# One engine makes both parts of the filler weights, eight chunks ahead, in a one-core two-layer kernel

## The reference

```python
h = rms_norm(x, w)
swa_q, swa_k, swa_v, swa_gate, mla_q, c_kv, k_rope, mla_gate, mem_q, mem_gate = split(h @ w_in)
out_swa = attention(norm(swa_q), norm(swa_k), swa_v, bias, window) * silu(swa_gate)
kv      = rms_norm(c_kv, kv_norm) @ w_kv_up
out_mla = attention(rope(norm(mla_q)), rope(norm([kv, k_rope])), kv) * silu(mla_gate)
out_mem = attention(norm(mem_q), norm(mem @ w_k), mem @ w_v) * silu(mem_gate)
x = x + concat(out_swa, out_mla, out_mem) @ w_out
```

## Time and profile before

| | us |
|---|---|
| median of 3 runs | 2868.59 (2864.26 to 2870.82) |
| profiled execution, whole time | 2862.06 |
| its span | 2860.3 |
| PE busy | 2573.9 |
| DVE busy | 1334.4 |
| ACT busy | 1087.0 |
| POOL busy | 511.7 |

### The profile page before, as it was taken

How to read it: one execution, slowest core, us unless ns; L and a number is a source line. 1 busy time by engine, 2 the same in 40 slices (tenths; PEclk the granted TensorE clock), 3 DMA queues, 4 the chain that set the end, 5 groups by cost and what they waited for, 6 DMA issues and landing times. The chain is left out here.

```text
span 2860.3 us, 39591 instructions
## 1 busy us (share of the span) xinstructions
PE 2573.9 (90%) x14740; PEld 1873.2 (65%) x14740; DVE 1334.4 (47%) x2501; ACT 1087.0 (38%) x1922; POOL 511.7 (18%) x411
## 2 busy tenths in 40 slices
PE   8999999998888889999989999677889988978888
PEld 7984556886544444459957768565678767756667
DVE  5654784664211112347745545533435433474443
ACT  5553122443222122235434224344445344434444
POOL 0000110020011100010000000555530065064332
PEclk9999999999999999999999999898899989999999
DMA  7754344553599999945420135322244533432332
GB/s 300 220 205 152 134 145 144 184 199 123 239 422 422 422 421 422 380 187 179 172 81 32 46 126 197 119 103 103 103 148 150 177 114 115 147 118 104 130 116 107
DMA packets 80320, 529.77 MB, mean 185 GB/s; under 512 B 9088, under 2 KB 13568, under 8 KB 18848
## 3 DMA queue, kind: packets, MB, share of 16 engines
q1 hardware_dynamic: 76128, 514.50, 47.5%
q0 software_dynamic: 3456, 11.02, 1.5%
q10 hardware_dynamic: 576, 2.10, 0.2%
HBM read 520.24 MB, written 7.34 MB: 184 GB/s over the span
## 5 line engine op out<-in xcount | busy, mean ns | idle before, releaser
L798 POOL TENSOR_TENSOR parts_wl<-ring,parts_wh 128x512 fp32r<-128x512 f32 x288 | 396.3, 1395 | 1160.8 <-ACT parts_wh L783 1156.0
L759 PE MATMUL ps<-parts_wh,layer_xh 128*128 128x512 f32 x576 | 251.6, 437 | 107.8 <-POOL parts_wl L798 45.1
L2302 PE MATMUL ps<-ring,yT 128*64 128x256 f32 x2048 | 247.7, 386 | 52.6 <-DMA ring<-in_weights 48.5
L783 ACT ACTIVATE parts_wh<-ring 128x512 fp32r<-128x512 f32 x288 | 175.9, 629 | 276.9 <-PE ps L761 260.5
L760 PE MATMUL ps<-parts_wl,layer_xh 128*128 128x512 f32 x576 | 240.1, 417 | 0.0
L761 PE MATMUL ps<-parts_wh,layer_xl 128*128 128x512 f32 x576 | 239.6, 416 | 0.0
L2302 PEld LDWEIGHTS ps<-ring,yT 128*64 128x64 f32 x2048 | 137.7, 137 | 155.6 <-DMA ring<-in_weights 91.2
L1169 PE MATMUL ps<-ring,xT 128*128 128x512 f32 x512 | 222.0, 592 | 2.8 <-PEq L488 1.7
L759 PEld LDWEIGHTS ps<-parts_wh,layer_xh 128*128 128x128 f32 x576 | 117.3, 204 | 149.4 <-issue 58.6
L413 DVE TENSOR_TENSOR split_wl<-ring,split_wh 128x512 fp32r<-128x512 f32 x208 | 145.3, 709 | 96.5 <-ACT split_wh L387 95.4
L456 ACT ACTIVATE features_wh<-ring 128x512 fp32r<-128x512 f32 x208 | 130.3, 631 | 133.3 <-PE ps L473 133.3
(11 more groups left out here) (671 smaller groups left out, 5328.9 us busy)
## 6 DMA issues: line engine op xcount, KB each, us to landing
ring<-in_weights SPq DMA_DIRECT2D x468, 1024.0 KB, 5.0
x_res<-in_x SPq DMA_DIRECT2D x1, 2048.0 KB, 7.6
yT<-in_mem SPq DMA_DIRECT2D x1, 2048.0 KB, 15.7
rel_skew<-lru_feat POOLq DMA_DIRECT2D x1, 2048.0 KB, 49.8
mem_features<-yT ACTq DMA_DIRECT2D x4, 512.0 KB, 6.9
s_wb<-in_s_bc POOLq DMA_DIRECT2D x4, 512.0 KB, 3.9
s_wc<-in_s_bc POOLq DMA_DIRECT2D x4, 512.0 KB, 3.9
gate_bias<-in_gate_bias POOLq DMA_DIRECT2D x8, 256.0 KB, 3.9
```

Source lines behind the costliest of these rows:

```text
L759: mm(out, xh[:, kc, at], wh[:, c, :], start=kc == 0, stop=False)
L783: k.nc.scalar.activation(k.parts[0][:, c, :], k.ring[:, slot, c * BLK:(c + 1) * BLK], ACT.Copy).then_inc(w_high.sem, 1)
L798: k.nc.gpsimd.tensor_tensor(k.parts[1][:, c, :], k.ring[:, slot, c * BLK:(c + 1) * BLK], k.parts[0][:, c, :], ALU.subtract)\
L2302: last = nc.tensor.matmul(k.ps[s * WIN:(s + 1) * WIN, p, 0:FF], window[:, p, kc, :], k.ring[:, slot, at:at + FF], start=kc == 0, stop=kc = ...
```

## The change

- `LEAD` and the depth of the high parts go from 4 to 8 chunks (`LATE_DEEP`), in the late `gemm_tokens` stages too. The low part is written over the raw chunk in the ring (`k.w_low` lies where the ring's four slots lie), so in those stages the slot is given back by PE's last use and no longer by DVE's.
- In `SplitFill`, ACT makes no high parts: GpSimd makes the high part, waits for it, and makes the low part. `highs` is empty.
- `SmallProduct` gives way to `KeyProduct`: 96 fp32r matmuls of 64 columns, run on PE inside `rms_scale`; GpSimd splits its weights beside the `gemm_tokens` stage.
- The `gemm_tokens` of 2 column blocks in `mla_branch` is gone. Its 32 steps go into the fills: the sliding-window fill has 80 steps (latent inputs 64, half of the gate 16), the latent fill 80 (16 of the gate, 64 as before).
- Steps by block: even layer 24, turns of 16, 16, 16 and 8, then 16, memory 8, turns of 8, 8. Sliding window 16, 8, turns of 12, 8. Latent 16, 16, turns of 8, 16. Odd memory 8, turns of 8, 8.
- In `attention`, DVE evicts a filler block of slot 1 after the mixing and no longer ahead of it; `head_norm` can evict one early.

```diff
-        wh, wl = (k.sb(scope, f"split_w{n}", [P, deep, BLK], F32R) for n in "hl") if parts is None else parts
+        deep = LATE_DEEP if late else SPLIT_DEEP
+        if not late:
+            wh, wl = (k.sb(scope, f"split_w{n}", [P, deep, BLK], F32R) for n in "hl")
 
         def raw(unit, turn, c):
             return k.ring[:, slot_of(unit, turn, 2 * upb), c * BLK:(c + 1) * BLK]
+
+        def high(j, kc):
+            return k.w_high[:, (j * chunks + kc) % deep, :] if late else wh[:, kc % deep, :]
+
+        def low(unit, turn, j, kc):
+            c = kc % UNIT_KC
+            return k.w_low[:, slot_of(unit, turn, 2 * upb), c * BLK:(c + 1) * BLK] if late else wl[:, kc % deep, :]
...
+                            if late and c == UNIT_KC - 1:
+                                mid.then_inc(k.unit_used, 1)
...
-                        dve.drain().then_inc(k.unit_used, 1)
+                            nc.vector.tensor_tensor(low(unit, turn, j, kc), raw(unit, turn, c), high(j, kc), ALU.subtract).then_inc(w_low.sem, 1)
+                        if not late:
+                            dve.drain().then_inc(k.unit_used, 1)
...
-    LEAD = SPLIT_DEEP
+    LEAD = LATE_DEEP
...
     def highs(self, act, steps):
-
-        if self.act_done < len(self.blocks):
-            self.make_highs(act, min(self.act_at + steps, self.first[self.act_done + 1] + self.LEAD))
-
-    def make_highs(self, act, upto):
-        k, x_high, w_high, w_used = self.k, self.k.ev("x_high"), self.k.ev("w_high"), self.k.ev("w_used")
-        for step in range(self.high_at, min(upto, self.total)):
-            while self.act_done < len(self.blocks) and self.first[self.act_done + 1] <= step - self.LEAD:
-                self.take_act(act)
-            act.wait_ge(w_used.sem, w_used.at(step - SPLIT_DEEP))
-            coming = self.raw_piece(step)
-            if coming is not None:
-                n, _, piece = coming
-                k.nc.scalar.activation(self.blocks[n][0][0][:, piece, :], self.blocks[n][4][:, piece, :], ACT.Copy).then_inc(x_high.sem, 1)
-            slot, c = unit_wait(k, act, self.base + step // UNIT_KC, 0, 0), step % UNIT_KC
-            k.nc.scalar.activation(k.parts[0][:, c, :], k.ring[:, slot, c * BLK:(c + 1) * BLK], ACT.Copy).then_inc(w_high.sem, 1)
-            self.high_at = step + 1
+        pass
 
     def lows(self, pool, steps):
-        k, x_high, x_low, w_high, w_low = (self.k, *(self.k.ev(n) for n in ("x_high", "x_low", "w_high", "w_low")))
+        k, copy, minus = self.k, self.k.nc.gpsimd.tensor_copy, self.k.nc.gpsimd.tensor_tensor
+        x_high, x_low, w_high, w_low, w_used = (k.ev(n) for n in ("x_high", "x_low", "w_high", "w_low", "w_used"))
         self.pool_at += steps
         for step in range(self.low_at, min(self.pool_at + self.LEAD, self.total)):
+            pool.wait_ge(w_used.sem, w_used.at(step - self.LEAD))
             coming = self.raw_piece(step)
             if coming is not None:
                 n, m, piece = coming
                 (xh, xl), raw = self.blocks[n][0], self.blocks[n][4]
+                copy(xh[:, piece, :], raw[:, piece, :]).then_inc(x_high.sem, 1)
                 pool.wait_ge(x_high.sem, x_high.at(m))
-                k.nc.gpsimd.tensor_tensor(xl[:, piece, :], raw[:, piece, :], xh[:, piece, :], ALU.subtract).then_inc(x_low.sem, 1)
-            slot, c = slot_of(self.base + step // UNIT_KC, 0, 0), step % UNIT_KC
+                minus(xl[:, piece, :], raw[:, piece, :], xh[:, piece, :], ALU.subtract).then_inc(x_low.sem, 1)
+            slot, c = unit_wait(k, pool, self.base + step // UNIT_KC, 0, 0), step % UNIT_KC
+            high, raw_w, at = k.w_high[:, step % self.LEAD, :], k.ring[:, slot, c * BLK:(c + 1) * BLK], slice(c * BLK, (c + 1) * BLK)
+            copy(high, raw_w).then_inc(w_high.sem, 1)
             pool.wait_ge(w_high.sem, w_high.at(step))
-            k.nc.gpsimd.tensor_tensor(k.parts[1][:, c, :], k.ring[:, slot, c * BLK:(c + 1) * BLK], k.parts[0][:, c, :], ALU.subtract)\
-                .then_inc(w_low.sem, 1)
+            minus(k.w_low[:, slot, at], raw_w, high, ALU.subtract).then_inc(w_low.sem, 1)
             self.low_at = step + 1
...
+    def split(self, pool):
+        k, high = self.k, self.k.ev("small_high")
+        pool.wait_ge(k.loaded, k.loads)
+        k.nc.gpsimd.tensor_copy(self.high[:, :, :], self.raw).then_inc(high.sem, 1)
+        pool.wait_ge(high.sem, high.at(0))
+        k.nc.gpsimd.tensor_tensor(self.low[:, :, :], self.raw, self.high[:, :, :], ALU.subtract)
 
     def multiply(self, pe, steps):
-        k, n, mm = self.k, self.n, self.k.ev("small_mm")
-        pe.wait_ge(k.loaded, k.loads)
+        k, n, mm, made = self.k, self.n, self.k.nc.tensor.matmul, self.k.ev("small_mm")
+        xh, xl = k.layer
         for t in range(NT):
+            out, at = k.ps[:, 0, t * n:(t + 1) * n], slice(t * P, (t + 1) * P)
             for kc in range(KC):
-                last = k.nc.tensor.matmul(k.ps[:, self.bank, t * n:(t + 1) * n], k.xT[:, kc, t * P:(t + 1) * P], self.w[:, kc, :],
-                                          start=kc == 0, stop=kc == KC - 1)
-        last.then_inc(mm.sem, 1)
+                mm(out, xh[:, kc, at], self.high[:, kc, :], start=kc == 0, stop=False)
+                mm(out, xh[:, kc, at], self.low[:, kc, :], start=False, stop=False)
+                last = mm(out, xl[:, kc, at], self.high[:, kc, :], start=False, stop=kc == KC - 1)
+        last.then_inc(made.sem, 1)
...
-              fill=fill, steps=(5, 4, 4, 3), turned=free.rearrange("p (j a) -> p j a", j=2))
+              fill=fill, steps=[(4, 4, 4, 4)] * 3 + [(3, 3, 1, 1)], turned=free.rearrange("p (j a) -> p j a", j=2))
...
-        gemm_tokens(k, None, 2, KC // UNIT_KC, *store_tokens(k, pq, 2 * BLK), whole=k.layer, parts=k.parts)
...
-            rms_scale(k, ckv, ckv, n=KV_RANK, squares=squares)
+            rms_scale(k, ckv, ckv, n=KV_RANK, squares=squares, fill=product)
```

206 lines of the change are left out of this document (101 added, 105 removed).

## The result

| | before | changed |
|---|---|---|
| median, us | 2866.4 (2861.4 to 2870.8, 4 runs) | 2957.8 (2954.8 to 2959.2, 4 runs) |
| ratio | 1 | 1.0318, 95% interval 1.0298 to 1.0338 |
| span of the profiled execution, us | 2860.3 | 2955.3 |

The account below looks back on a forecast made before the run. PE was taken to bound the kernel, with GpSimd pacing the head norms after the change; +147 - 62 - 47.5 - 5.5 + 7.5 = +39.5 us on the median of 2868.6 gave 2908 us, range 2852 to 2955.

Parts of the forecast that it names:

- The price of a step on GpSimd: In the fills: copy 0.57, hand-over 0.07, subtraction 1.26, together 1.90 us a step, bounds 1.78 and 2.59.
- 13 us: In the fills: a copy of 0.44 us by the engine reference would make the sum about 13 us smaller.
- The blocks paced by GpSimd: Head-norm blocks: GpSimd's steps at 1.90 us plus what DVE takes set their length, +147 us.
- The turns: Attention blocks: differential turn 30.5 us for about 38, DVE staging the next pair after 7.5 us; attention sum -62 us.
- rival 1: In ten attention turns, each of eight two-input DVE operations waits 0.7 us or more: about +30, 2938 us; chance 0.16.
- GpSimd waits about 7.5 us for the first filler step of each: Sliding-window attention and gate: that wait, then 24 steps at 1.90 us; 125 us, was 115.7, so +9.
- hidden: Attention blocks: GpSimd's work fits inside the block, as 121 us in the differential attention's 127.
- The key product: Old product off its stage, -5.5 us; 96 matmuls at 0.114 us inside the 4.3 us block, +7.5 us.
- Even memory attention: Even layer's memory block: 16 steps for 32, two turns of 20 and 18; 45 us, was 73.3, so -28.
- The removed stage, the late slots: The gemm_tokens of 32 steps goes, -47.5 us; later reloads into late slots cost nothing while DMA share stays near 0.5.
- Rival 2: In the fills: the copy costs as much as the subtraction, 2.59 us a step; 3095 us; chance 0.10.
- Rival 3: Attention turns fall to PE's own work as ACT has nothing to make, with cheaper GpSimd steps: -76, 2832 us; chance 0.15.

Follow-up runs that it names:

- Experiment 5: Changed kernel with GpSimd's copy cut to 64 of 512 columns from the ninth step of each fill on: 2887.7 us, ratio 1.0079.
- experiment 8: Changed kernel with GpSimd beginning a turn's parts only once DVE has staged the next pair: 2933.8 us; the same wait added to act_highs: 2822.1 us.
- experiment 9: Changed kernel with the old float32 key product in the stage before: 2946.6 us; or with the new product's operands exchanged, 48 matmuls of 256 columns: 2944.5 us.
- act_highs: Changed kernel with the high parts given back to ACT, GpSimd making only the low parts: 2830.4 us, ratio 0.9876.

## Why the prediction was wrong in size and right in sign

**The price of a step on GpSimd: right.** Copy 0.61 us for 0.57, subtraction 1.28 for 1.26, 1.90 to 1.94 from start to start for 1.90. The estimate of 0.44 us from the GPSIMD Engine Reference of the Trainium skill (section 3, on performance versus the Vector engine) was without the fixed cost. Experiment 5 agrees with the page's price of an element (0.84 ns measured, 1.03 cycles at 1.2 GHz are an estimated 0.86) and adds about 0.18 us of fixed cost, which together give the 0.61. The "13 us" that the prediction put on that estimate was wrong in itself: 0.13 us on 144 to 192 steps are 19 to 25 us.

**The blocks paced by GpSimd: right.** 69.4, 71.4, 92.6 and 35.1 us for 69, 71, 93 and 34.5; together 268.5 for 267.5. (The items of the prediction give 70.2 and 92.4 where it wrote 71 and 93, so the rounding helped by a microsecond.) Only the two last even head norms came out 5.5 us longer (63.5 for 58). "n x 1.90 plus what DVE takes" is a sound way to cost such a block.

**The turns: the term that failed.** The step was "DVE has staged the next pair 7.5 us after its first scale": I took DVE's chain at its old length into a turn in which GpSimd works nearly all the time. It is 11.9 us in the turn shown. In the differential attention the mean of the staged keys went from 0.42 us to 1.05, of the negation from 0.17 to 0.71. PE then waits 3.33 + 1.50 us for the staging and 0.7 more ahead of the filler behind the probabilities, and is busy for about 2 us longer at a granted clock of 0.91: 36.2 for 30.5. Over all turns PE waits 36.8 us for the staging where it waited 3.5.

This is the mechanism of rival 1, to which I gave 0.16, and experiment 8 shows it. Its form was not quite as I wrote. Of the "eight two-input operations" only the four of the staging waited in the turn shown; the mixing took 3.0 us, as in the fastest turn of before, because GpSimd stood from 1912.3 to 1916.4 there and waited for PE. The negation, which has one input and wasn't on the list, waited in their place. What I held against the rival, "four of the eight are staging, ahead of a wait of only about 1 us", was wrong: the staging is what PE waits for next, so a wait of 1 us is all the cover there is. The SBUF — State Buffer page of the Trainium skill (section "Who interferes with whom") says that a DVE instruction with two SBUF inputs contends with a GpSimd instruction that reads SBUF, and that a reduction never does; the trace agrees with both, 1.49 us for 0.42 and 1.22 us as before.

Four rows carry the miss: differential attention +11.2 us, sliding window +11.6, latent +19.2, odd memory +1.9. Experiment 8 takes back 3.7, 2.4, 14.0 and 2.4 of them. So the staging is shown as the cause in the latent and odd memory rows and for a part of the differential one. The sliding-window row failed by another step, "GpSimd waits about 7.5 us for the first filler step of each": GpSimd is the last to end in both of its attention blocks, and it stood for 12.1 and 14.0 us of them until PE had used chunks, which is 11 us more than the forecast had. PE used them late, and stood for 6.2 us inside the turns for the staging; but with the staging undisturbed GpSimd's waits were as long (12.3 and 12.1 us), since the wait of experiment 8 itself holds it back.

**The end of the attention blocks.** I wrote "hidden" where GpSimd needs less than the block. Its last eight steps begin only when PE gives back chunks, so it ends late all the same: PE stands for 6.33 us at the barrier after the latent attention and 6.9 us between the two blocks of the sliding-window attention, with GpSimd the last to end (0.2 and 0.5 us ahead of the barrier, PE 6.0 and 5.9). Before the change PE was through 4.8 and 2.2 us ahead of the same barriers; over the six attention blocks it is 25.2 us for 17.1. PE's timeline in the changed kernel, at the first of them:

```profile
2745.84 0.77 PE L764 MATMUL ps<-late_wh,layer_xh 128*128 128x512 f32 x1 [6.33 <-PEq L2813]
```

**The key product: mis-sized.** +7.5 us was the estimate, +12.8 came (4.3 to 17.1). 0.11 us for a matmul was right for the first 41; from there on the granted clock was 0.50 and it was 0.21 us, which the estimate left out. In six profiled executions that have the narrow product the clock fell after 21 to 41 of its 96 matmuls, and the product took 16.5 to 18.5 us. The old one gave back 4.5 us (121.7 to 117.2 for its stage) of the 5.5 forecast, so the move cost 8.3 us net by the blocks and 11.2 by the medians (experiment 9).

**Even memory attention (44.3 for 45): in part luck.** PE waits 3.1 us for the staging in its turn as well, which the forecast didn't have, and the row came out all the same.

**The removed stage, the late slots: right.** DMA shares stay at 0.24 to 0.37 in the fills, the late `gemm_tokens` stages are as long as before (25.8 us for 26.0, 48.6 for 48.8 and 29.4 for 29.4), and PE's largest wait for weights is 48.1 us where it was 48.5, in a stage that the change leaves alone.

**What remains.** Against the forecast the blocks sum to +54.8 us. Experiment 8 takes back 23.9 of them, the key product is 5.1, the last even head norms 5.5. The other 20 lie in the sliding window (9.2), the differential attention (7.5) and the latent attention (5.2), less small gains elsewhere. GpSimd's longer waits in the sliding window, the mixing and the later ends of the blocks are what the traces show at these places; no run took them away one by one, so their shares stay open.

**The other rivals.** Rival 2 (the copy as dear as the subtraction, 3095) falls by the rows above. Rival 3 (faster, 2832) named the right gain, ACT's order: `act_highs` has it, at 2830. In the changed kernel what GpSimd pays is more than that.

## What to carry to other kernels

When work goes to an engine that another one has to wait for, cost it twice: its own time, and every short instruction of the other engine that now meets it. Here each waited for at most the rest of the GpSimd instruction that was running (a subtraction of 1.28 us made 0.17 into 1.04). Look at what the next engine waits for: six short operations of one chain paid 4.4 us between them, and PE stood for most of it. Then look at what the long stream will meet if it is moved. A wait that kept GpSimd from running beside the staging made the kernel faster by 24 us and took no work away, but the stream met the mixing in its place and gave a part of it back.

## What the runs showed of the hardware

- DVE's operation on 128x4 values: 0.17 us alone, 1.04 beside GpSimd's subtraction, ending 0.03 us after the end of it.
- GpSimd's copy of f32 to fp32r: 0.61 us for 512 columns, 0.24 for 64 (medians); beside DVE's squaring in the head norm 1.6 us for 512.
- An fp32r matmul of 64 columns on weights of 128x128 has the same start-to-start time as one of 256 columns on weights of 128x64, 0.11 us at 2.4 GHz; after 41 of the narrow ones the granted clock fell to 1.2 GHz though PE had not paused. In six profiled executions it fell after 21 to 41 of them.
